# Opening of the projection stage: the weight matrix split in two column groups, the first block normalised on one engine, the first latents taken slice by slice

## What is computed

```python
x = _layer_norm(x, ln_in_g, ln_in_b)
proj = jnp.einsum('bsd,df->bsf', x, w_in)          # 1024 -> 512 + 384 + 256 + 32
pool_out = _pool_mixer(proj[..., :o1], w_pool, pool_scale)
attn_out = _mla(proj[..., o1:o2], proj[..., o2:o3], proj[..., o3:], q_norm_g, w_uq, kv_norm_g, w_ukv)
```

## Time and profile before

| what | us |
|---|---|
| median of three runs | 1418.12 |
| lowest and highest run | 1415.09, 1421.05 |
| the profiled execution, its own time | 1419.5 |
| its span in the trace | 1417.2 |
| projection stage, from the start to PE's last matmul | about 230 |
| PE busy, DVE busy, ACT busy over the span | 1205.8, 958.2, 714.0 |

### The profile page before, as it was taken

One profiled execution on the slowest core, in us unless ns is written; L12 is line 12 of the kernel. 1 busy time (PEld: TensorE's weight loads), 2 busy tenths in 40 slices (PEclk: granted clock), 3 DMA queues, 4 the chain that ended last, 5 costly groups with the idle time before them and its releaser, 6 DMA issues. The chain is left out here.

```text
span 1417.2 us, 22002 instructions
## 1 busy us (share of the span) xinstructions
PE 1205.8 (85%) x7370; PEld 1075.7 (76%) x7370; DVE 958.2 (68%) x1541; ACT 714.0 (50%) x1213; POOL 382.2 (27%) x437
## 2 busy tenths in 40 slices
PE   3999995688899899894999992699999999999950
PEld 3999994467687687783777871699999999999950
DVE  7545433888778777784645678477777777777746
ACT  4222222556667676673322213466666766666634
POOL 2223310455420000000122214234433343333317
PEclk9999998799999999997999996899999999999985
DMA  7333324433220100004854461788998889988747
GB/s 266 123 112 111 111 83 150 148 127 49 66 51 7 42 11 11 5 12 144 246 168 149 149 240 57 223 252 275 264 281 269 256 278 264 284 273 258 203 119 265
DMA packets 160368, 226.84 MB, mean 160 GB/s; under 512 B 25281, under 2 KB 125377, under 8 KB 160321
## 3 DMA queue, kind: packets, MB, share of 16 engines
q1 hardware_dynamic: 150464, 191.64, 42.0%
q0 software_dynamic: 9856, 34.61, 9.9%
HBM read 171.12 MB, written 55.10 MB: 160 GB/s over the span
## 5 line engine op out<-in xcount | busy, mean ns | idle before, releaser
L2073 PE MATMUL ps_gate_up<-xT_hi_lo,w_hi 128*128 128x384 f32 x896 | 261.3, 356 | 1.4 <-DVE xT_hi_lo L1998 1.4
L2074 PE MATMUL ps_gate_up<-xT_hi_lo,w_lo 128*128 128x192 f32 x896 | 224.5, 251 | 0.0
L1993 DVE TENSOR_TENSOR w_lo<-w_raw,w_hi 128x2048 fp32r<-128x2048 f32 x93 | 212.3, 2282 | 0.0
L1933 ACT ACTIVATE w_hi<-w_raw 128x2048 fp32r<-128x2048 f32 x92 | 175.7, 1910 | 0.0
L2074 PEld LDWEIGHTS ps_gate_up<-xT_hi_lo,w_lo 128*128 128x128 f32 x896 | 170.7, 191 | 0.6
L2073 PEld LDWEIGHTS ps_gate_up<-xT_hi_lo,w_hi 128*128 128x128 f32 x896 | 168.7, 188 | 2.2 <-issue 1.6
L795 ACT ACTIVATE pT_hi<-ps_probsT 128x512 fp32r<-128x512 f32 x160 | 87.0, 596 | 62.3 <-PE ps_probsT L1032 62.2
L804 ACT ACTIVATE probs<-ps_scores,neg_max 128x1024 f32<-128x1024 f32 (+1 forms) x96 | 93.1, 974 | 43.8 <-DVE neg_max L909 43.2
L1849 POOL TENSOR_TENSOR d_wait_carrier<-d_zero 128x1 f32<-128x1 f32 x78 | 36.9, 473 | 285.7 <-PE ps_xT L2062 147.9
L909 DVE TENSOR_REDUCE neg_max<-ps_scores 128x1 f32<-128x1024 f32 (+1 forms) x80 | 97.0, 1213 | 22.8 <-PE ps_scores L83 22.8
L922 DVE TENSOR_TENSOR pT_lo<-ps_probsT,pT_hi 128x512 fp32r<-128x512 f32 x160 | 101.3, 672 | 5.6 <-ACT pT_hi L795 5.5
(11 more groups left out here) (258 smaller groups left out, 3239.5 us busy)
## 6 DMA issues: line engine op xcount, KB each, us to landing
w_raw<-in_w_gate SPq DMA_DIRECT2D x32, 1024.0 KB, 8.2
w_raw<-in_w_up SPq DMA_DIRECT2D x32, 1024.0 KB, 8.6
w_raw<-in_w_down SPq DMA_DIRECT2D x32, 1024.0 KB, 6.9
scratch_x<-x SPq DMA_DIRECT2D x24, 512.0 KB, 5.1
x_again<-scratch_x SPq DMA_DIRECT2D x12, 512.0 KB, 3.4
scratch_acc<-acc_out SPq DMA_DIRECT2D x12, 512.0 KB, 3.1
w_raw<-scratch_acc SPq DMA_DIRECT2D x12, 512.0 KB, 6.6
w_in_raw<-in_w_in SPq DMA_DIRECT2D x8, 592.0 KB, 9.3
```

The costliest lines, as they stand in the source:

```text
L1933: act.activation(w_hi[c][:, :], raw[:, c, :], ACT.Copy).then_inc(hi_done, 1)
L1993: nc.vector.tensor_tensor(w_lo[c][:, :], raw[:, c, :], f32(w_hi[c][:, :]), ALU.subtract).then_inc(lo_done, 1)
L2073: nc.tensor.matmul(ps[:, 0:2 * N], w_hi[chunk][:, at], xT[:, k, :], start=k == 0, stop=False)
L2074: nc.tensor.matmul(ps[:, 0:N], w_lo[chunk][:, at], xT[:, k, 0:N], start=False, stop=False)
```

## The change

It makes one ring of five full slices into 18 pieces: 8 latents pieces (672 columns of a slice), 8 pooling pieces (512 columns), 2 value pieces. All 8 latents pieces have a place of their own and are loaded first; a pooling piece or value piece takes the place of an earlier piece, after its rest was taken. The two rotary tables are loaded between the latents and the pooling pieces, the two small vectors of gains between the pooling and the value pieces. The second tile of x is loaded behind gain and bias. In block 0, DVE does the whole normalisation in two instructions per tile, (x - mean) * gain and then * deviation + bias, and POOL no longer adds the bias there. DVE's order becomes: first tile's statistics, normalisation, second tile's statistics, rest of latents piece 0, rest of the first transposed tile, second tile's normalisation, the other rests, with the second transposed tile's after piece 5. PE computes the very first latents slice by slice, both column groups of a slice together, and the first `pool_inputs` waits piece by piece. PE's loop of two passes is written out.

```diff
-        RING = 5
-        w_raw = m.sb("w_in_raw", [P, RING, IN_DIM])
+        LAT, SPLITS = IN_DIM - POOL_DIM, 2 * KD + KVT_
+        w_raw = m.sb("w_in_raw", [P, KD * LAT])
...
-        X0T_AFTER = (3, 6)
+        X0T_AFTER = (1, 5)
+
+        def part(c):
+
+            if c < KD:
+                at, cols, k = c * LAT, slice(POOL_DIM, IN_DIM), c
+            elif c < 2 * KD:
+                at, cols, k = (c - KD) * POOL_DIM, slice(0, POOL_DIM), c - KD
+            else:
+                at, cols, k = KD * POOL_DIM + (c - 2 * KD) * 512, slice(0, 512), c - 2 * KD
...
             def load_w(c):
-                if c >= RING:
-                    sp.wait_ge(w_lo_done, c - RING + 1)
+                if c >= KD:
+                    sp.wait_ge(w_lo_done, c - KD + 1)
...
+            load_x(dram["x_sample"][0:P, :], 0)
             for dst, name in ((ln_g, "ln_in_g"), (ln_b, "ln_in_b")):
                 sp.dma_start(dst[:, :], dram[name].partition_broadcast(P)).then_inc(ln_loaded, 16)
-            for c in range(RING):
+            load_x(dram["x_sample"][P:2 * P, :], 1)
+            for c in range(KD):
                 load_w(c)
             sp.dma_start(rope_cos[:, :, :], dram["rope_cos"]).then_inc(consts_loaded, 16)
             sp.dma_start(rope_sin[:, :, :], dram["rope_sin"]).then_inc(consts_loaded, 16)
+            for c in range(KD, 2 * KD):
+                load_w(c)
             with nc.allow_non_contiguous_dma("a gain per partition, once"):
                 sp.dma_start(q_g[:, :], dram["q_norm_g"].rearrange("(t p) -> p t", p=P)).then_inc(consts_loaded, 16)
                 sp.dma_start(kv_g[:, :], dram["kv_norm_g"].rearrange("(t p) -> p t", p=P)).then_inc(consts_loaded, 16)
-            for c in range(RING, KD + KVT_):
+            for c in range(2 * KD, SPLITS):
                 load_w(c)
...
             pool.wait_ge(ln_loaded, 32)
-            for s in range(2):
-                add_bias(0, s)
...
+            def normalise_first(s):
+                dve.wait_ge(stats_done, s + 1)
+                nc.vector.scalar_tensor_tensor(out=x0[:, s, :], in0=x_in[:, s, :], scalar=moments[:, s, 0:1], in1=ln_g[:, :],
+                                               op0=ALU.subtract, op1=ALU.mult).then_inc(x_centred, 1)
+                dve.wait_ge(rstd_done, s + 1)
+                dve.wait_ge(x_centred, s + 1)
+                nc.vector.scalar_tensor_tensor(out=x0[:, s, :], in0=x0[:, s, :], scalar=rstd[:, s:s + 1], in1=ln_b[:, :],
+                                               op0=ALU.mult, op1=ALU.add).then_inc(x0_done, 1)
...
+            statistics(0, 0)
             dve.wait_ge(filled, 4)
             dve.wait_ge(ln_loaded, 32)
...
+            normalise_first(0)
+            statistics(0, 1)
+            rest_w(0)
+            rest_x0T(0, 0, 0)
+            normalise_first(1)
+            for c in range(1, SPLITS):
+                rest_w(c)
+                if c == X0T_AFTER[1]:
+                    rest_x0T(0, 1, 0)
             dve.wait_ge(consts_loaded, 64)
...
+                if isinstance(t, int) and t == 0:
+                    for k in range(KD):
+                        pe.wait_ge(w_lo_done, k + 1)
+                        for h, (c0, c1) in enumerate(halves):
+                            last = three_passes(nc, ps_lat[h][:, 0:c1 - c0], x0T_hi[slot][:, k, 0:P], x0T_lo[slot][:, k, 0:P],
+                                                w_hi[:, k, c0:c1], w_lo[:, k, c0:c1], k == 0, k == KD - 1)
...
+                        if first and h == 0 and g == 0:
+                            pe.wait_ge(w_lo_done, KD + k + 1)
...
-            with pe.Fori(0, PAIRS - 1) as i:
+            step(0, first=True)
+            for i in range(1, PAIRS - 1):
                 step(i)
             step(PAIRS - 1, last=True)
```

More of the change, by code:

```diff
@@ L133, in phase_project @@
         consts_loaded, ln_loaded = m.sem("a_consts_loaded"), m.sem("a_ln_loaded")
-        w_loaded = [m.sem(f"a_w_loaded{s}") for s in range(RING)]
+        w_loaded = [m.sem(f"a_w_loaded{s}") for s in range(KD)]
         w_hi_done, w_lo_done = m.sem("a_w_hi_done"), m.sem("a_w_lo_done")
@@ L152, in phase_project @@
         PAIRS = N_BLOCKS // 2
-        X0T_AFTER = (3, 6)
+        X0T_AFTER = (1, 5)
[6 more added lines that the diff above has]
+                at, cols, k = KD * POOL_DIM + (c - 2 * KD) * 512, slice(0, 512), c - 2 * KD
+            hi, lo = (w_hi, w_lo) if c < 2 * KD else (wv_hi, wv_lo)
+            size = cols.stop - cols.start
+            return w_raw[:, at:at + size], hi[:, k, cols], lo[:, k, cols]
         SPLIT = Q_RANK
@@ L240, in add_bias @@
             def add_bias(j, s):
-                pool.wait_ge(x_scaled, 2 * j + s + 1)
+                pool.wait_ge(x_scaled, 2 * j + s - 1)
                 pool.tensor_tensor(x0[:, s, :], x0[:, s, :], ln_b[:, :], ALU.add).then_inc(x0_done, 1)
@@ L280, in round_x0T @@
                                    ps_tr[h][:, :].rearrange("p (k t) -> p k t", t=P), ACT.Copy).then_inc(tr_hi_done, 1)
[L282 to L287, removed]
+            for c in range(SPLITS):
+                raw, hi, _ = part(c)
+                act.wait_ge(w_loaded[c % KD], 16 * (c // KD + 1))
+                act.activation(hi, raw, ACT.Copy).then_inc(w_hi_done, 1)
                 if c in X0T_AFTER:
@@ L398, in scale_latT, with rest_w @@
                                         ALU.subtract).then_inc(kv_lo_done, 1)
-            for s in range(2):
-                statistics(0, s)
+            def normalise_first(s):
[6 more added lines that the diff above has]
+                                               op0=ALU.mult, op1=ALU.add).then_inc(x0_done, 1)
+            def rest_w(c):
+                raw, hi, lo = part(c)
+                dve.wait_ge(w_hi_done, c + 1)
+                nc.vector.tensor_tensor(lo, raw, f32(hi), ALU.subtract).then_inc(w_lo_done, 1)
+            statistics(0, 0)
             dve.wait_ge(filled, 4)
             dve.wait_ge(ln_loaded, 32)
[L404 to L415, removed]
+            normalise_first(0)
[7 more added lines that the diff above has]
+                    rest_x0T(0, 1, 0)
             dve.wait_ge(consts_loaded, 64)
@@ L458, in latents @@
                 pe.wait_ge(kr_products, 2 * t)
-                for h, (c0, c1) in enumerate(((POOL_DIM, POOL_DIM + SPLIT), (POOL_DIM + SPLIT, IN_DIM))):
+                halves = ((POOL_DIM, POOL_DIM + SPLIT), (POOL_DIM + SPLIT, IN_DIM))
+                if isinstance(t, int) and t == 0:
[4 more added lines that the diff above has]
+                                                w_hi[:, k, c0:c1], w_lo[:, k, c0:c1], k == 0, k == KD - 1)
+                            if k == KD - 1:
+                                last.then_inc(lat_done, 1)
+                    return
+                for h, (c0, c1) in enumerate(halves):
                     if s == 0 and not (isinstance(j, int) and j == 0):
@@ L462, in latents @@
                     for k in range(KD):
-                        if isinstance(t, int) and t == 0 and h == 0:
-                            pe.wait_ge(w_lo_done, k + 1)
                         a_hi, a_lo = (x[slot][:, k, s * P:(s + 1) * P] for x in (x0T_hi, x0T_lo))
@@ L468, in latents, with pool_inputs @@
                     last.then_inc(lat_done, 1)
-            def pool_inputs(j, h, slot):
+            def pool_inputs(j, h, slot, first=False):
                 pe.wait_ge(u_copied, 2 * j)
@@ L495, in values @@
                 if isinstance(j, int) or s == 0:
-                    pe.wait_ge(w_lo_done, KD + KVT_)
+                    pe.wait_ge(w_lo_done, SPLITS)
                 pe.wait_ge(kv_lo_done, 2 * j + s + 1)
@@ L506, in _, with step @@
             latents(0, 0, 0)
-            def step(i, last=False):
+            def step(i, last=False, first=False):
                 for b in range(2):
@@ L512, in step @@
                     pe.wait_ge(tr_lo_done, 4 * j + 4)
-                    pool_inputs(j, 0, b)
+                    pool_inputs(j, 0, b, first=first and b == 0)
                     transpose_latents(j, 0)
```

10 lines of the change are left out of this document (5 added, 5 removed).

## The result

The changed kernel took 1427.81 us (median of 20 runs), the kernel before 1420.97 (20 runs beside them): ratio 1.005, 95% interval 1.0035 to 1.0065, so **7.1 us slower** (5.0 to 9.2). +1.2 was forecast. The direction was right; the sum was too small, and the time lies above the range, which ended at 1423.8.

The account below looks back on a forecast made before the run. The prediction took block 0's hand-over from DVE to PE, at 42 us, as the bound. DVE's entry (-0.6) and the clock behind PE's pause (+1.8) made +1.2 on 1418.1, 1419.3 us; range 1414.8 to 1423.8.

Parts of the forecast that it names:

- the sum: Whole kernel: -0.6 for DVE's earlier entry and +1.8 for the clock make +1.2 us, 1419.3 us.
- a term held at nothing: Costed at nothing: PE's loop written out, as one jump fewer, with the last pass straight already.
- PE's side: Block 0: PE starts the latents at 20.3, ends the pooling half at 35.4, some 6.5 us ahead of 41.97.
- rival 1: Behind block 0's hand-over: PE's lead carries through, the 6.5 us stay, 1411.6 us; chance 0.07.
- DVE's side: Block 0: DVE enters its first pass at 32.7 instead of 33.26; PE's hand-over moves from 41.97 to 41.4.
- The -0.6: Block 0: the gain in us from DVE entering its first pass at 32.7 instead of 33.26.
- What the pause costs: Block 0: PE stands from 35.4 to 41.4, then runs at half rate for 3.2 to 4.0 us; 1.8 lost.
- rival 3: Opening loads: small vectors hold up the value pieces, DVE enters 3.5 to 4.8 late; 5.3 to 6.6 slower; chance 0.09.
- rival 4: Opening loads: each smaller load pays its own fixed time, 2.8; all behind 12 late, about 1432; chance 0.02.
- rival 2: Behind PE's pause in block 0: the clock stays up, the pause costs nothing, 1416 to 1417.5 us; chance 0.17.

Follow-up runs that it names:

- the second profile: The changed kernel, unaltered, profiled and timed once more against the kernel before: ratio 1.0042 (1.0024 to 1.006).
- the first run: The changed kernel with PE's loop over the first two passes put back, timed against the kernel before: ratio 1.0031 (1.0012 to 1.0049).

## Why the prediction fell short

Two steps failed. One is a term held at nothing, PE's loop written out; the other is the wait for the next x, which the prediction left out of DVE's entry.

- *PE's side* was right: 20.3 forecast for the latents and 20.5 measured, 35.4 for the pooling half's end and 35.4. That this lead is worth nothing (rival 1 against the forecast) was right. The turned order shows why, by the profiles: with DVE's scaling ahead of the next block's statistics the hand-over comes at 36.03 with the early latents and at 39.23 without. The times don't tell these two apart.
- *DVE's side* was right to 0.2 us up to the last rest (32.7 and 32.9). The step that failed next is "The new x for it is issued right after, near 28, as before (its issue is not what DVE waited for)". The issue did come near 28, at 28.34. But the load landed 1.9 later than before, at 33.8, and so DVE entered at 34.06. Its wait for x was 1.13 here, 1.08 in the second profile and 2.53 with the loop. The -0.6 became +0.7 in the first profile, nothing in the second (hand-over 41.96) and +1.9 with the loop. Why that load took 5.5 us instead of 4.2 stays open: with the value pieces out of its way it took 6.5.
- *What the pause costs* was right in its mechanism and about right in size: 1.8 lost by the forecast. Half rate lasted 5.1 us in the first profile, 3.1 in the second and 3.4 with the loop, so 2.6, 1.6 and 1.7 were lost. With the hand-over these make 3.3, 1.6 and 3.6, and block 0 ended 3.1, 1.5 and 3.6 later than before. With PE kept busy the clock stayed up, and block 0 ended sooner by 2.3 (straight code) and, the hand-over taken off, by 1.7 (loop).
- *A price from a page*: the Trainium skill ("DMA: Bandwidth & Descriptors", section Anatomy of one DMA) fits a transfer on the GpSimd path by about 2.0 us and its bytes at 436 GB/s, an estimate of 2.6 us for 256 KB. The value pieces, which SP issues, took 3.8 in the median, so that fit is not to be carried over to them; the rows of before, 4.0 in the middle, were the better guide.
- *At nothing* held the term that was most wrong: "PE's loop written out: it is one jump fewer, and the last pass was straight already". Alone it costs 3.8 us (0.9 to 6.7). A straight last pass said nothing on it: its code is loaded once either way, and the two passes in front of it take four loads more when they are written out (11 instead of 7). What I didn't look for in the trace of before is the row of instruction loads, and what lies beside them.
- *The sum*: 3.8 for the loop and 4.4 for the rest (the first run) make 8.2, inside the 5.0 to 9.2 measured, if the two simply add, which no run tests. Of the 4.4 the profiles show 1.5 to 3.6 at the end of block 0. So the direction came out right for the reason given, the clock, but by these numbers about half of the loss came from a term that the sum didn't have.
- *Rivals*: the small vectors (rival 3) landed in 2.6, so their 10.5 was the queue's. Loads of 336 KB in a queue paid no time of their own (rival 4): the last pooling piece, which waits for the eighth latents rest, was issued by 25.8, where by rival 4 the eighth latents piece itself would land only near 37. The piece that rival 4 calls lone was not: it was issued at 27.06, before the other one, issued at 24.56, had landed (29.2), so what a lone load needs is not shown. The clock fell, against rival 2. The range's upper end, 1423.8, was to be rival 3's near end, which is 1423.4 by its own sum; the time lies above both.

Left open: how 3.8 us come of the loads of code. The long issues are shown, and one of them is followed above through x and DVE to PE's wait. PE's later waits are longer by 1.0 in sum with the loop alone, and by 2.6 and 1.0 in the changed kernel's two profiles. In three of the four profiles with such issues the clock fell once in a later block, worth 1.5 or so; but it fell once in three profiles with the loop too (before, DVE's normalisation alone, the loop kept busy), so this isn't shown to come of the loads.

## What to carry over

An engine's lead is worth what the next hand-over lets through: before moving loads and weights forward, follow the other engine's queue up to the first point where the two meet, and see what it does there for somebody else. Here turning round the order of steps inside the pass was worth some 11 us with the old loads (and block 0 normalised on DVE, which alone showed no gain by the ratio), and the change with the old order cost 7. And count code as a transfer: a loop written out is loaded piece by piece, beside whatever else is moving.

## What the hardware showed unexpectedly

Loading instructions (16 KB or so at a time, on a queue of its own) went with a longer issue of SP's two loads of x whenever the two met behind the opening, nine times of nine: 1.06 to 2.19 us instead of 0.83 to 0.96. Moving all of PE's code by 108 instructions (54 matmuls with their weight loads) moved the meetings. And a pause of PE near 2 to 4 us is not a safe guide to the clock: it fell behind 1.87 (before), 1.81, 2.28, 3.06 and 3.98 us and stayed up behind 2.02 and 3.41. With DVE's normalisation alone it stayed up behind 1.81 at 75.00 us and fell behind 1.81 at 142.88, in one profile.
